# Two-layer transformer kernel on one Trainium2 core: ScalarE rounds the first eight weight units, angles, bias and distances leave the opening's VectorE list, projection quarters spread over 24 iterations

## What is computed

```python
for l in range(2):
    proj = rms_norm(x, attn_norm[l]) @ w_in[l]              # 1024 -> 416 + 1152 + 768 columns
    o_mla  = latent attention, 6 heads, with rotary angles cos/sin(pos * inv_freq)
    # differential attention, 6 heads, two score maps each:
    s = q k^T * scale - slope * |pos_q - pos_k|;  masked by 64-chunk causality
    o_diff = (softmax(s0) - lam * softmax(s1)) @ v
    # chunk attention, 4 heads: softmax(q k^T / 8 + rel_bias) @ v, same mask
    x = x + concat(o_mla, o_diff, o_ch) @ w_out[l]
    x = x + conv_ffn(rms_norm(x, ffn_norm[l]))
```

## Time and profile before

| | us |
|---|---|
| median of three runs | 2936.36 |
| lowest and highest | 2934.60, 2937.76 |
| the profiled execution, its own time | 2937.29 |
| its span in the trace | 2935.6 |
| PE busy in the span | 2872.3 (98%) |
| DVE, ACT, POOL busy | 1368.2, 845.5, 1364.7 |

### The profile page before, as it was taken

One profiled execution on the slowest core, in us unless ns is written; L12 is line 12 of the kernel. 1 busy time (PEld: TensorE's weight loads), 2 busy tenths in 40 slices (PEclk: granted clock), 3 DMA queues, 4 the chain that ended last, 5 costly groups with the idle time before them and its releaser, 6 DMA issues.

```text
span 2935.6 us, 40700 instructions
## 1 busy us (share of the span) xinstructions
PE 2872.3 (98%) x14014; PEld 2378.2 (81%) x14014; DVE 1368.2 (47%) x2969; ACT 845.5 (29%) x1901; POOL 1364.7 (46%) x924
## 2 busy tenths in 40 slices
PE   7999999999999999999999999999999999999998
PEld 6777888888778888879888878888798888788886
DVE  6665524265665534354772541112647735411124
ACT  3463302123462211123552231001225532300012
POOL 5313555565214455555233645555352336455553
PEclk9999999999999999999999999999999999999999
DMA  7313555565315565555333746565463336555653
GB/s 271 122 55 133 188 193 193 193 219 190 101 44 180 183 203 191 195 196 181 108 121 132 225 155 208 193 194 193 141 204 108 116 129 223 171 194 187 200 192 109
DMA packets 136520, 494.15 MB, mean 168 GB/s; under 512 B 15280, under 2 KB 15536, under 8 KB 136112
## 3 DMA queue, kind: packets, MB, share of 16 engines
q0 software_dynamic: 66240, 241.20, 25.6%
q1 hardware_dynamic: 68544, 245.40, 24.7%
q10 hardware_dynamic: 1584, 5.46, 0.5%
HBM read 489.91 MB, written 2.10 MB: 168 GB/s over the span
## 4 chain that ended last, share of the span: by engine, by line
PE 68%; DVE 1%; ACT 1%; issue 0%; POOL 0%; DVEq 0%; POOLq 0%; ACTq 0%
PE ps L576 18%; PE ps L578 18%; PE ps L577 18%; PE ps L847 2%; PE ps L604 2%; PE ps L600 2%; PE ps L601 2%; PE ps L839 1%; PE ps L828 1%; PE ps L723 1%; PE ps L725 1%; PE ps L724 1%; PE ps L829 1%; PE ps L1069 0%; DVE tmp L1662 0%
## 5 line engine op out<-in xcount | busy, mean ns | idle before, releaser
L549 POOL TENSOR_TENSOR w_lo<-w_raw,w_hi 128x1024 fp32r<-128x1024 f32 x460 | 1107.8, 2408 | 99.9 <-DMA w_hi<-weights 90.2
L576 PE MATMUL ps<-hi,w_hi 128*128 128x512 f32 x2920 | 1151.6, 394 | 1.2 <-POOL w_lo L549 1.1
L578 PE MATMUL ps<-lo,w_hi 128*128 128x512 f32 x2920 | 1140.8, 391 | 0.0
L577 PE MATMUL ps<-hi,w_lo 128*128 128x512 f32 x2920 | 1140.6, 391 | 0.0
L544 POOL DMA_DIRECT2D w_hi<-weights x460 | 261.2, 568 | 1436.5 <-PE ps L578 1028.0
L576 PEld LDWEIGHTS ps<-hi,w_hi 128*128 128x128 f32 x2920 | 550.3, 188 | 122.3 <-issue 10.8
L578 PEld LDWEIGHTS ps<-lo,w_hi 128*128 128x128 f32 x2920 | 549.8, 188 | 116.3
L577 PEld LDWEIGHTS ps<-hi,w_lo 128*128 128x128 f32 x2920 | 550.2, 188 | 108.0 <-issue 1.0
L2067 ACT ACTIVATE ps<-hb,col 128x512 f32<-128x512 f32 x88 | 68.5, 782 | 381.1 <-DVE hb L1204 381.1
L1810 DVE SCALAR_TENSOR_TENSOR x<-x,ps 128x512 f32<-128x512 f32 x64 | 43.3, 686 | 257.0 <-PE ps L578 194.4
L2215 ACT ACTIVATE sq<-ps 128x512 f32<-128x512 f32 x64 | 38.2, 597 | 380.0 <-PE ps L604 231.0
(11 more groups left out here) (351 smaller groups left out, 3611.0 us busy)
## 6 DMA issues: line engine op xcount, KB each, us to landing
w_raw<-weights SPq DMA_DIRECT2D x460, 512.0 KB, 3.3
w_hi<-weights POOLq DMA_DIRECT2D x460, 512.0 KB, 3.7
x<-xt SPq DMA_DIRECT2D x8, 256.0 KB, 10.0
out<-x SPq DMA_DIRECT2D x8, 256.0 KB, 2.0
kc<-k ACTq DMA_DIRECT2D x1, 1346.0 KB, 6.2
bias<-relb ACTq DMA_DIRECT2D x2, 512.0 KB, 4.9
bias<-relb ACTq DMA_DIRECT2D x1, 1024.0 KB, 5.0
praw<-pt ACTq DMA_DIRECT2D x2, 512.0 KB, 5.7
```

What stands on the lines that cost most here:

```text
L549: nc.gpsimd.tensor_tensor(wlo[s][:, :], raw[s][:, :], whi[s][:, :].bitcast(F32), ALU.subtract).then_inc(w_split, 1)
L576: nc.tensor.matmul(out_ap, w[0], xx[0], start=first, stop=False)
L577: nc.tensor.matmul(out_ap, w[1], xx[0], start=False, stop=False)
L578: return nc.tensor.matmul(out_ap, w[0], xx[1], start=False, stop=last)
```

## The change

What it does, in the order of the diff:

- ScalarE makes `whi` of units 0 to 7 with a Copy from `raw` (`own_high`), in place of the loads by GpSimd's queue: unit 0 first of all its work, unit 1 after chunk 1 of `hi`, unit 2 after chunk 5, unit 3 after chunk 7, units 4 and 5 after the squares, unit 6 after the root, unit 7 after the copy of rx. GpSimd's own loads begin with unit 8.
- VectorE subtracts unit 0; GpSimd subtracts unit 1 in two pieces (two chunks, then six), and all others.
- The first chunk columns of `col` come in a small DMA of their own ahead of kc1 (`gain_in`); the dummy product runs twice and waits for kc1 alone (`k1_in`). The sum of squares is gathered in bank 3 instead of bank 7.
- In layer 0 TensorE's sums of squares run behind unit 2 and the spread behind unit 3 (before: ahead of unit 2 and behind it).
- The sign of the distances is turned (the score's scale is negative), so that only a 64x64 corner of each needs the mask; the bias is scaled on ScalarE in iterations 11 and 13 and VectorE adds the mask to a 64x4x64 corner in iteration 16, in both layers.
- `angles()` is cut into three parts, in iterations 2, 4 and 6 of layer 0's loop; sine and cosine on ScalarE in iteration 9; signed sine in iteration 12. ScalarE's exponential for lambda stands behind the copies of the first values, in both layers.
- Quarters: one instead of two in iterations 4, 8, 12, 16, and two in 22 and 23. The order of the projections, `AT_STATS` (12 to 20), `AT_TURN`, `AT_SPREAD`, the first two items and the times of two squares move with it.

The core of the diff:

```diff
-ITEM_AT = {28: "Q0", 29: "K0", 31: "V0", ...
+ITEM_AT = {29: "Q0", 30: "K0", 31: "V0", ...
-FULL = ["dq1", "dk1", "cc0", "cc1", "cc2", "dq2", "dk2", "cq0", "ck0", "cq1", "ck1"]
+FULL = ["dq1", "dk1", "cc0", "dq2", "dk2", "cc1", "cc2", "cq0", "ck0", "cq1", "ck1"]
...
-        QUARTERS = {it: 2 for it in range(22)}
+        QUARTERS = {it: 1 if it in (4, 8, 12, 16) else 2 for it in range(24)}
...
+        ANGLES_AT, AT_SINE, AT_BIAS = (2, 4, 6), 9, 11
-        AT_STATS, AT_TURN, AT_SPREAD, AT_KR = 12, 22, 24, 29
+        AT_STATS, AT_TURN, AT_SPREAD, AT_KR = 20, 24, 25, 29
-        SQUARE_AT = {14: (0, 8), 21: (1, 16), 29: (2, 24), 37: ...
+        SQUARE_AT = {22: (0, 8), 25: (1, 16), 30: (2, 24), 37: ...
...
-            for s in range(2):
-                load_high(s, 0, True)
-            for s in range(2):
-                low_half(s, 0)
-            for s in range(2, RING):
-                load_high(s, 0, True)
-            low_half(2, 0)
-            with pool.Fori(1, N_UNITS // RING) as i:
+            pool.wait_ge(w_hi_made, 2)
+            subtract(1, slice(0, 2 * P)).then_inc(w_second, 1)
+            pool.wait_ge(w_first, 1)
+            subtract(1, slice(2 * P, UNIT)).then_inc(w_split, 2)
+            for u in range(2, OWN_HIGH - 1):
+                pool.wait_ge(w_hi_made, u + 1)
+                subtract(u % RING).then_inc(w_split, 1)
+            load_high(0, OWN_HIGH // RING)
+            pool.wait_ge(w_hi_made, OWN_HIGH)
+            subtract(RING - 1).then_inc(w_split, 1)
+            for s in range(1, RING):
+                load_high(s, OWN_HIGH // RING)
+                low_half(s - 1, OWN_HIGH // RING)
+            with pool.Fori(OWN_HIGH // RING + 1, N_UNITS // RING) as i:
...
                     for kc in range(lead):
                         chunk_of(1, kc)
+                    if q.unit == 0:
+                        pe.wait_ge(w_split, 2)
...
-            pe.wait_ge(par_in, 48)
-            keep_busy(1, kc1[:, 0:S])
+            pe.wait_ge(k1_in, 16)
+            keep_busy(2, kc1[:, 0:S])
...
-                first_sums()
-                values((2, 2, 2, 2), 384, A, need, natural, first_spread)
+                if l:
+                    first_sums()
+                values((2, 2, 2, 2), 384, A, need, natural, {0: first_spread} if l else {0: first_sums, 1: first_spread})
...
-            dve.wait_ge(par_in, 48)
+            dve.wait_ge(w_hi_made, 1)
+            V.tensor_tensor(wlo[0][:, :], raw[0][:, :], whi[0][:, :].bitcast(F32), ALU.subtract).then_inc(w_first, 1)
+            dve.wait_ge(gain_in, 16)
             for c in range(NC_):
                 prep_low(c, lambda c: pcol("attn_norm", 0, c), (hi[0], lo[0]))
...
-                for h in range(CH_H):
-                    last = V.scalar_tensor_tensor(out=bias[:, h, :], in0=bias[:, h, :], scalar=CH_HD ** 0.5,
-                                                  in1=kc1[:, 0:S], op0=ALU.mult, op1=ALU.add)
-                link(last)
...
                 def side(it):
+                    if l == 0 and it in ANGLES_AT:
+                        angles(ANGLES_AT.index(it))
+                    elif l == 0 and it == AT_SINE + 3:
+                        signed_sine()
+                    elif it == AT_BIAS + 5:
+                        bias_masked()
...
+            def own_high(u):
+
+                act.wait_ge(w_loaded[u % RING], 16 * (u // RING) + 16)
+                if u >= RING:
+                    act.wait_ge(w_used, u - RING + 1)
+                A_(whi[u % RING][:, :], raw[u % RING][:, :], ACT.Copy).then_inc(w_hi_made, 1)
...
                     A_(dst[0][:, c, :], x[:, c, :], ACT.Copy, scale=gain(c)).then_inc(hi_ready, 1)
+                    if not ready and c in (1, 5, 7):
+                        own_high({1: 1, 5: 2, 7: 3}[c])
...
-            act.wait_ge(par_in, 48)
+            own_high(0)
+            act.wait_ge(gain_in, 16)
             prep(lambda c: pcol("attn_norm", 0, c), (hi[0], lo[0]), ready=False)
+            for u in range(RING, RING + 2):
+                own_high(u)
...
+                    if it in (AT_BIAS, AT_BIAS + 2):
+                        h = it - AT_BIAS
+                        act.wait_ge(aux_in, 32 + 16 * l)
+                        A_(bias[:, h:h + 2, :], bias[:, h:h + 2, :], ACT.Copy, scale=CH_HD ** 0.5).then_inc(bias_scaled, 1)
+                    elif l == 0 and it == AT_SINE:
+                        act.wait_ge(tab_ready, 3)
+                        A_(sin1[R, :], sin1[R, :], ACT.Sin).then_inc(tab_act, 1)
+                        A_(cos1[R, :], cos1[R, :], ACT.Sin).then_inc(tab_act, 1)
```

131 lines of the change are left out of this document (79 added, 52 removed).

## The result

The changed kernel is slower: 2946.22 us in the median against 2938.61 us, a ratio of 1.0026 with an interval of 1.0017 to 1.0036. That is 7.6 us lost where 3.1 us were forecast as a gain, and 5.7 us beyond the upper end of the range. The profiled execution of after took 2950.34 us, at the long end of its own.

The account below looks back on a forecast made before the run. TensorE, busy 2872.3 of 2935.6 us, bounds the kernel; only its idle 63.3 us and clock can be won. Terms -3.0 + 3.5 + 0.3 - 1.6 - 2.6 + 0.3 = -3.1 us: 2933.3 us, range 2926.0 to 2940.5.

Parts of the forecast that it names:

- the clock: TensorE's half-clock stretch at 40 to 50 us in the opening: no gain counted, bounds 0 and 1.5 us.
- the opening: Layer 0 up to the second group of values: 3.0 us gained, bounds 1.5 and 5.5.
- the two loops: Attention loops of the first network: +3.5 and +0.3 lost in layer 0, -1.6 and -2.6 gained, +0.3 lost in layer 1.
- Start and dense products: Opening of layer 0: first real product at 8.4 to 8.8 us, dense ends at 21.1 against 24.2, 3.1 us gained.
- The root: Opening of layer 0: root and reciprocal done at 33.0 us against 30.7 before, bounds 30.7 and 34.1; TensorE waits 2.5 us.
- The second group: Second group of values, layer 0's opening: starts at 43.5 us against 46.5, with 0.7 us of idle instead of 2.1.
- Angles: Layer 0's loop, iterations 2, 4 and 6: 5.6 us of added VectorE work costs 3.5 us, bounds 0.5 and 6.
- The sines: Layer 0's loop, iteration 9: sine and cosine with table loads take ScalarE 3.8 us; 0.3 us lost, 0 to 2.
- The third rival: Iterations 4 to 9 of layer 0: VectorE falls behind, 2940.8 to 2943.4 us; chance 0.10.
- Bias: Both attention loops: two ScalarE scalings of 1.06 us and the 0.3 us corner fit the engines' gaps and cost nothing.
- Stats and quarters: Both loops: 1.6 us gained from moving the sums to iteration 20, 2.6 from quarters in 22 and 23 (bounds 0 and 4).
- the second rival: Iterations 22 to 28: VectorE sets the pace, the quarters pay nothing and idle moves on; 2935.9 us; chance 0.17.

Follow-up runs that it names:

- with the bias later: Changed kernel with ScalarE's two bias scalings in iterations 15 and 17 instead of 11 and 13: 2949.41 us, ratio 1.0041.
- plan alone: Kernel before with only the new loop plan (quarters, projection order, sums, items, squares); opening, angles and bias as before: 2936.51 us, ratio 0.9997.
- the new opening alone: Changed kernel with the old loop plan and angles and sines back in the opening, no tiny loads: 2946.52 us, ratio 1.0031.
- bias later: In the table: new opening and old loop plan, angles and sines in the opening, bias in iterations 15 and 17, mask in 20: ratio 0.9999.
- angles and sines in the opening: Changed kernel with angles, sines and signed sine moved from the loop back to the opening: 2940.44 us, ratio 1.0006.
- angles spread: Changed kernel with the eleven angle steps one to an iteration (5 to 18) and the sines in iteration 19: 2939.30 us, ratio 1.0005.
- changed kernel, tiny loads: Changed kernel with eight two-column loads added to GpSimd's queue and its loop split: 2942.19 us, ratio 1.0012.
- plan, items later, tiny loads: Kernel before with the new loop plan, V0 and Q1 to V2 an iteration later, eight tiny loads: 2935.14 us (0.9979), then 2930.75 us (0.9971).
- everything, bias in 5 and 7: New opening and loop plan, angles and sines in the opening, four items later, eight tiny loads, bias in 5 and 7, mask in 10: 2930.92 us, 0.9974.

## Why the prediction was wrong

**The step that failed is the clock.** The sum counts idle time and puts the granted clock at nothing: "I count no gain, with bounds of 0 and 1.5", and that for one place. The lost clock grew by 6 us in the mean of the executions (25.3 to 31.3), twice the whole forecast and the other way. At full clock the change costs 1.4 us where 3.1 were forecast as a gain. TensorE's idle did fall, by 1.0 us in the two traces: the opening gave 3.6 (3.0 forecast), but the two loops took 2.9 where the sum had -0.1, since the quarters gave less than forecast. Why the clock falls more often in the changed kernel no run shows.

**Start and dense products: a little beyond the bound.** Dense ended at 22.8 us where 21.1 was forecast and 22.3 was the bound; the wait was 0.5 us for lo instead of 1.4 for unit 1. The first twelve products took 4.6 us (9.07 to 13.69) and not the 2.7 of the sum, which used 0.227 us for each; the first seven start 0.4 to 1.1 us apart (in before the first five 0.4 to 0.6).

**The root: beyond the upper bound.** 34.64 us instead of 33.0 (bound 34.1). The stand-still that I counted on the distances fell on a cast of four numbers (2.24 us), which I had not priced.

**The second group: late by the root and the clock.** I took "no gain, bounds 0 and 1.5", as if the old low stretch simply stayed. It went from 47 us to 36 us, right behind the spread, and cost 1.7 us there; with the late root that used up the 3.0 us at this point. What I had not counted is that the old stretch behind the group was gone, so 1.5 us came back up to the first scores. In the executions without a stretch behind the spread, the first scores lie 3.0 us earlier than in the kernel before. That is the number forecast, but by luck: the group starts 1.6 us earlier there (44.9 us) and not 3.0, and the other 1.5 are the clock.

**Angles: about right.** The waits are 3.1 us (3.5 forecast), and two of the stand-stills fell about where I put them. The sines brought 1.2 us (0.3 forecast, bound 2); the 0.5 us at 119.9 us is not theirs alone, for it is there in layer 1 and with the sines in the opening too. Moving all this back takes 4.0 us of idle out of the loop, against 3.8 in the sum. The time fell by 5.9 us, uncertain by 4; that the 2 us over are more than noise is not shown. The third rival, VectorE falling behind, is the one whose time came; its condition (waits over 10 us in iterations 4 to 12) did not: they were 4.8 us up to 120 us. So it is not the mechanism.

Between the table loads of the sines and their neighbours the trace leaves 0.02 us (load 100.30 with 1.28 us, sine 101.60; load 102.76, exponential 104.06). The drain of 1.4 us beside each load that the Trainium skill, page "ScalarE: Activation LUTs", section "What ACT_TABLE_LOAD costs", speaks of is not seen here either, and the sum was right to leave it out.

**Bias: costed at nothing; wrong for the old plan.** "The engines' gaps there are 1 us and 3 us" was true of ScalarE's list and said nothing of what is queued behind the copy. In the changed plan it is a wait of 0.5 us, which is gone in layer 1 with the bias later; with the old plan it is 0.94 us ahead of the sums, twice, and more behind them.

**Stats and quarters: the waits went, and others came.** 0.81 us twice and 0.64 and 0.92 us (and 0.90) went as forecast, and 1.14 and 0.94 us in each layer with them. The term was 3.9 us of gain; the plan alone takes 2.2 us of idle out of the two loops. What the sum left out is that idle comes back further on: I priced `ITEM_AT` at nothing, where Q0 and K0 come an iteration later and V0 and Q1 do not. Ahead of V0, behind VectorE's work on Q0, there are 1.85 us, and ahead of Q1 1.09 us, in each layer. But this line is not the whole of it, for with V0 and Q1 later too 1.56 and 1.03 us come at other places, and the idle of the loops stays. That is the second rival's mechanism, the idle moving on, for half of the term.

**Not in the sum at all: 3.4 us** in the 2060 us that I had declared untouched. Eight loads taken from GpSimd's queue shift its later pauses against the rest of the code. "Almost all" of the idle in the first 50 us and the two loops was misread as well: 26.7 of the 63.3 us lie in this rest, 10.4 of them behind the last product. Its row with `issue` and 6.33 us at 715 us, and its fellows at 1450, 2126 and 2810 us, were in the trace of before.

The terms depend on the kernel in which they are taken, so they are read along a path. Before to plan alone -0.9 us, the new opening into it +2.6 (the moved pause included), angles and sines into the loop +5.9: that is the 7.6 measured. Along another, the new opening alone +9.1 (with the bias ahead of the sums), the plan into it -7.3, angles and sines +5.9. Each step is uncertain by some 4 us.

Time against the kernel before in the same series, means of all executions, taken apart into lost clock and what is left:

| kernel | lost clock, us | left, us |
|---|---|---|
| changed kernel | +6.0 | +1.4 |
| plan alone | +1.4 | -3.5 |
| opening alone; bias later | +7.6; +2.8 | +0.6; -3.1 |
| angles and sines in the opening | +4.7 | -3.4 |
| angles spread | +4.9 | -3.2 |
| changed kernel, tiny loads | +3.1 | +1.0 |
| plan, items later, tiny loads, twice | -3.2; -2.0 | -2.3; -5.4 |
| everything, bias in 5 and 7 | -1.9 | -5.9 |

The two series of one kernel in the next to last row show how far a figure can be trusted: to 3 us. (For the changed kernel, the five series of the kernel before together stand in for its own, which has no clocks on record.) Within that, moving angles and sines back is time at full clock (-4.8 us), and the tiny loads are clock (-2.9 us).

## What to carry to other kernels

When a sum of waits is made for a kernel that is 98% busy, look at the mean granted clock of all executions beside the time: here it moved by more than the waits did. When a piece of a schedule is moved, walk the resource that its neighbours share (here the PSUM banks of V0 and Q1), not only the engine that does it, and count idle over the whole loop, since a wait that goes can come back further on. When a change alters how many loads a queue issues, code far behind it can fall out of step with the others: cut both traces at fixed places and compare the untouched rest first. Work taken off a list pays only if it was on the path there, and a free gap in the new list is free only for an operation that fits into it singly, at its blocked length.

## What was not expected of the hardware

- GpSimd pauses ahead of a load at regular counts (113, 223, 333, 443 loads before it, in both traces of the kernel before and in the nine others with its loop). At the third of them in before the chain holds 3.15 us in which nothing visible is waited for. With eight small loads and the loop split the later counts were 173 and 283 (new opening) or 181 and 291 (old opening). What causes it was not found.
- An operation of VectorE with one SBUF input is blocked by GpSimd's subtraction as those with two are: 0.26 us became 2.26, 0.42 became 2.30, and a cast of four numbers took 2.24. It is VectorE that waits even where its recorded start is first: in after, the first of the two operations at 1532.67 us began 0.21 us ahead of the subtraction and took 3.12 us in place of 0.69.
- The granted clock falls to its lower level in pieces that cost 1.7 us each, in the loops mostly near waits of 1 to 2 us or runs of tiny products, and the same code loses one to six such pieces in a row: the changed kernel's loop of layer 0 took 190.1 us, and 184.5 us in the kernel with the eight loads, which come only behind this loop.
- The mean granted clock differs from kernel to kernel (0.9884 to 0.9925 in the kernels here) at the same products, and with it the time: 0.97 us for each us of lost clock among 126 executions of one kernel.
